# Expert outputs of a mixture layer: two accumulators by column halves in place of two by block parity

## The reference

```python
def expert_block(args):
    tok, e = args
    xb = x2d[tok]
    hb = jax.nn.silu(xb @ exp_w1[e]) * (xb @ exp_w3[e])
    return hb @ exp_w2[e]

yb = lax.map(expert_block, (slot_tok.reshape(NB, MOE_BLOCK), block_expert))
routed = jax.ops.segment_sum(yb.reshape(P, D) * slot_w[:, None].astype(x2d.dtype), slot_tok, num_segments=N)
shared = (jax.nn.silu(x2d @ shared_w1) * (x2d @ shared_w3)) @ shared_w2
return routed + shared
```

## Time and profile before

| | us |
|---|---|
| median of 3 runs | 2030.21 |
| lowest and highest | 2025.59, 2031.33 |
| the profiled execution | 2026.94 |
| its span, first to last instruction | 2025.1 |

### The profile page before, as it was taken

How to read it: one execution, slowest core, us unless ns; L and a number is a source line. 1 busy time by engine, 2 the same in 40 slices (tenths; PEclk the granted TensorE clock), 3 DMA queues, 4 the chain that set the end, 5 groups by cost and what they waited for, 6 DMA issues and landing times.

```text
span 2025.1 us, 34620 instructions
## 1 busy us (share of the span) xinstructions
PE 1843.0 (91%) x9251; PEld 1421.6 (70%) x9251; DVE 1491.4 (74%) x2060; ACT 1262.7 (62%) x1746; POOL 734.3 (36%) x754
## 2 busy tenths in 40 slices
PE   5787998999999899599999999999999999999950
PEld 2343444799888555387888888888888888888840
DVE  3367555532668668854999999999999999999946
ACT  3353545443224333334888888888888888888842
POOL 3211000000003114533455555555555555555532
PEclk8898999999999999799999999999999999999985
DMA  7733210234302322526886998976777878997977
GB/s 240 262 128 114 78 36 21 83 117 140 88 1 84 130 92 97 219 95 228 289 299 163 320 347 264 334 248 152 220 268 236 275 273 303 324 326 279 312 220 186
DMA packets 121260, 399.55 MB, mean 197 GB/s; under 512 B 28397, under 2 KB 52973, under 8 KB 96237
## 3 DMA queue, kind: packets, MB, share of 16 engines
q1 hardware_dynamic: 75644, 281.66, 37.6%
q0 software_dynamic: 45264, 117.06, 22.1%
q10 hardware_dynamic: 290, 0.02, 0.0%
HBM read 355.47 MB, written 84.60 MB: 217 GB/s over the span
## 4 chain that ended last, share of the span: by engine, by line
PE 49%; DMA 3%; DVE 2%; issue 1%; ACT 1%; POOL 1%; ACTq 1%; DVEq 0%; SPq 0%; POOLq 0%
PE bank L1989 28%; PE bank L2009 14%; PE bank L1976 5%; DMA y<-yacc_scratch 1%; PE bank L1996 1%; DMA big<-in_exp_w 1%; ACT wuph L2086 1%; DVE big L2296 1%; ACTq L1744 0%; POOL slot_table L1918 0%; DVE big L2288 0%; DVE wupl L2181 0%; DVE y L2287 0%; DMA yacc_scratch<-y,idx_s 0%; DMA xg<-hn_scratch 0%
## 5 line engine op out<-in xcount | busy, mean ns | idle before, releaser
L2181 DVE TENSOR_TENSOR wupl<-big,wuph 128x2048 fp32r<-128x2048 f32 x214 | 489.9, 2290 | 74.9 <-ACT wuph L2086 71.3
L2086 ACT ACTIVATE wuph<-big 128x2048 fp32r (+1 forms) x214 | 408.7, 1911 | 11.8 <-SPq L1807 7.1
L1989 PE MATMUL bank<-wuph,xTh 128*128 128x512 f32 x912 | 366.0, 401 | 7.2 <-DVE xTl L2203 6.8
L1989 PE MATMUL bank<-wuph,xTl 128*128 128x512 f32 x912 | 358.3, 393 | 0.0
L1989 PE MATMUL bank<-wupl,xTh 128*128 128x512 f32 x912 | 356.8, 391 | 0.0
L1910 POOL DMA_INDIRECT yacc_scratch<-y,idx_s x105 | 227.4, 2166 | 301.8 <-ACT y L2077 285.2
L1900 POOL DMA_INDIRECT xg<-hn_scratch,idx_g x108 | 237.0, 2194 | 117.5 <-issue 109.4
L2189 DVE TENSOR_TENSOR w2l<-w,w2h 128x1024 fp32r<-128x1024 f32 x212 | 249.7, 1219 | 8.8 <-ACT w2h L2095 8.4
L2095 ACT ACTIVATE w2h<-w 128x1024 fp32r (+1 forms) x212 | 213.1, 1053 | 69.0 <-issue 59.0
L1989 PEld LDWEIGHTS bank<-wuph,xTh 128*128 128x128 f32 x912 | 172.2, 189 | 44.2 <-issue 6.4
L1989 PEld LDWEIGHTS bank<-wuph,xTl 128*128 128x128 f32 x912 | 171.6, 188 | 37.1
(11 more groups left out here) (360 smaller groups left out, 3153.4 us busy)
## 6 DMA issues: line engine op xcount, KB each, us to landing
big<-in_exp_w SPq DMA_DIRECT2D x128, 1024.0 KB, 9.8
w<-in_exp_w SPq DMA_DIRECT2D x64, 1024.0 KB, 11.7
wada<-in_w_ada POOLq DMA_DIRECT2D x16, 1024.0 KB, 6.3
wg<-in_w_in SPq DMA_DIRECT2D x14, 1024.0 KB, 5.3
wada<-in_w_ada SPq DMA_DIRECT2D x4, 2048.0 KB, 14.6
big<-in_w_in SPq DMA_DIRECT2D x8, 1024.0 KB, 5.4
yacc_scratch<-in_consts SPq DMA_DIRECT2D x9, 512.0 KB, 9.7
x<-x_scratch SPq DMA_DIRECT2D x9, 512.0 KB, 4.1
```

What stands on the lines that cost most here:

```text
L1989: mm = pe.matmul(b_up[j][:, :], x[:, k, :], w[:, :, k, :], start=(k == 0 and i == 0), stop=(k == KT - 1 and i == 2))
L2086: act.activation(part13(wup[j][0], half), raw13(e % WSLOT, half), ACT.Copy).then_inc(w_high, 1)
L2181: dve.tensor_tensor(part13(wup[j][1], half), raw13(e % WSLOT, half), part13(wup[j][0], half).bitcast(F32), ALU.subtract).then_inc(w_low, 1)
```

## The change

The two accumulators become 1152 x 512: the first holds columns 0 to 511 of every token, the second columns 512 to 1023. Each block is scattered by two indirect DMAs, one per half. All blocks now add into both tensors, so each of these DMAs waits until the same half of the block before has landed. The shared expert's outputs are stored in halves too, and nothing is filled with zeros. At the end SP loads each tile in two halves, and there is no adding load. ACT waits for both halves before it writes `y[j]` again, and in its last block down_high goes ahead of ht.

```diff
-            for t in range(NT):
-                sp.dma_start(m.yacc[1][t * P:(t + 1) * P, :], a["consts"][:, C_ZERO:C_END]).then_inc(m.s_zero, 16)
...
+        COLS = [slice(h * 512, (h + 1) * 512) for h in range(2)]
...
-            sp.wait_ge(y_out[0], n * 16 + 16 * ((NSH + 1) // 2))
+            for h in range(2):
+                sp.wait_ge(y_out[h], n * 32 + 16 * (NSH + 1))
             for t in range(NT):
-                sp.dma_start(y6[t][:, :], m.yacc[0][t * P:(t + 1) * P, :]).then_inc(s_y[min(batch_of(t), 1)], 16)
+                for h in range(2):
+                    sp.dma_start(y6[t][:, COLS[h]], m.yacc[h][t * P:(t + 1) * P, :]).then_inc(s_y[batch_of(t)], 16)
...
             def store(b):
 
                 hold(y_act, b + 2)
-                pool.dma_start(m.yacc[0][b * P:(b + 1) * P, :], y[b % 2][:, :]).then_inc(y_out[b % 2], 16)
+                for h in range(2):
+                    if b >= 1:
+                        hold(y_out[h], 16 * b)
+                    pool.dma_start(m.yacc[h][b * P:(b + 1) * P, :], y[b % 2][:, COLS[h]]).then_inc(y_out[h], 16)
 
             def scatter(q, j):
                 hold(y_act, q + (NSH + 2))
-                pool.indirect_dma_start(m.yacc[j], bass.IndirectOffsetOnAxis(ap=idx_s[j][:, :], axis=0), y[j][:, :], None,
-                                        compute_op=ALU.add, bounds_check=N - 1, oob_is_err=False).then_inc(y_out[j], 16)
+                for h in range(2):
+                    hold(y_out[h], q * 16 + 16 * NSH)
+                    pool.indirect_dma_start(m.yacc[h], bass.IndirectOffsetOnAxis(ap=idx_s[j][:, :], axis=0), y[j][:, COLS[h]], None,
+                                            compute_op=ALU.add, bounds_check=N - 1, oob_is_err=False).then_inc(y_out[h], 16)
...
-            pool.wait_ge(m.s_zero, 16 * NT)
...
-                    hold(y_out[j], r * 16 + 16 * ((NSH + u) // 2))
+                    hold(y_out[1], (r * 2 + u) * 16 + 16 * (NSH - 1))
...
-            hold(y_out[1], n * 16 + 16 * ((NSH + 1) // 2))
-            for j, (t0, t1) in enumerate(YPARTS):
-                if j < 2:
-                    pool.wait_ge(s_y[j], 16 if j == 0 else 16 * (NT - 1))
-                for t in range(t0, t1):
-                    pool.dma_start(y6[t][:, :], m.yacc[1][t * P:(t + 1) * P, :], accum_op=ALU.add).then_inc(s_sum[j], 16)
...
-            def y_half(b, j, sent):
+            def y_half(b, j):
                 act.wait_ge(down_done, 2 * b + 2)
                 if not (isinstance(b, int) and b < 2):
-                    act.wait_ge(y_out[j], sent * 16)
+                    for h in range(2):
+                        act.wait_ge(y_out[h], b * 16 - 16)
...
+            down_high(n * 2 + NSH, n * 2)
             ht(n * 2 + NSH)
-            down_high(n * 2 + NSH, n * 2)
...
-                dve.wait_ge(s_sum[batch_of(t)], 16 * (t1 - t0))
+                dve.wait_ge(s_y[batch_of(t)], 32 * (t1 - t0))
...
-        m.yacc = [dram(f"yacc_scratch{j}", (N, D)) for j in range(2)]
+        m.yacc = [dram(f"yacc_scratch{h}", (N, D // 2)) for h in range(2)]
```

More of the change, by code:

```diff
@@ L57 @@
 C_TAB = C_COL + NE
-C_ZERO = C_TAB + 2 * NCOL
-C_END = C_ZERO + D
+C_END = C_TAB + 2 * NCOL
 def shape_constants():
@@ L85, in shape_constants @@
     col = np.concatenate([np.sin(ca), np.cos(ca)], -1).astype(np.float32)
-    slots = c[:, C_TAB:C_ZERO].view(np.int32).reshape(P, NCOL, 2)
+    slots = c[:, C_TAB:C_END].view(np.int32).reshape(P, NCOL, 2)
     slots[:, :, 0] = N + np.arange(P, dtype=np.int32)[:, None]
-    c[:, C_TAB:C_ZERO] = slots.reshape(P, 2 * NCOL).view(np.float32)
+    c[:, C_TAB:C_END] = slots.reshape(P, 2 * NCOL).view(np.float32)
     return c, row, col
@@ L530, in _ @@
         def _(sp):
-            sp.dma_start(m.table, a["consts"][:, C_TAB:C_ZERO].bitcast(I32).rearrange("p (c w) -> p c w", w=2)).then_inc(m.s_table, 16)
+            sp.dma_start(m.table, a["consts"][:, C_TAB:C_END].bitcast(I32).rearrange("p (c w) -> p c w", w=2)).then_inc(m.s_table, 16)
             for g in range(2, 6):
@@ L1712, in stage_experts @@
             "h_turned", "hT_ready", "down_done", "y_copied", "pool_step"))
-        y_out = [sem(f"y_sent{j}") for j in range(2)]
+        y_out = [sem(f"y_sent{h}") for h in range(2)]
+        COLS = [slice(h * 512, (h + 1) * 512) for h in range(2)]
         gathered = m.gathered
-        s_y, s_out = [sem(f"ld_y6_{j}") for j in range(2)], sem("st_y")
-        s_sum = [sem(f"sum_y6_{j}") for j in range(4)]
+        s_out, s_y = sem("st_y"), [sem(f"ld_y6_{j}") for j in range(4)]
         x_new, x_sq, y_new, rooted = (sem(n) for n in ("x3_new", "x3_sq", "y_new", "rooted"))
@@ L1950, in _ @@
                     scatter(r * 2 + u, j)
-            hold(y_out[NSH % 2], n * 16 + 16 * (NSH // 2))
+            hold(y_out[1], n * 32 + 16 * (NSH - 1))
             tokens(n * 2, idx_s[NSH % 2])
@@ L2127, in _ @@
                 if b >= 1:
-                    y_half(b - 1, (b - 1) % 2, (b - 1) // 2)
+                    y_half(b - 1, (b - 1) % 2)
                 silu(b + 1, (b + 1) % 2)
@@ L2142, in _ @@
                     high(r * 2 + (u + NSH + 2), j, r * 2 + (u + 2), HALVES[1:2])
-                    y_half(r * 2 + (u + NSH - 1), 1 - j, r + (u + NSH - 1) // 2)
+                    y_half(r * 2 + (u + NSH - 1), 1 - j)
                     silu(r * 2 + (u + NSH + 1), 1 - j)
                     xt(r * 2 + (u + NSH + 2), j)
+            down_high(n * 2 + NSH, n * 2)
             ht(n * 2 + NSH)
-            down_high(n * 2 + NSH, n * 2)
-            y_half(n * 2 + (NSH - 1), 1 - NSH % 2, n + (NSH - 1) // 2)
-            y_half(n * 2 + NSH, NSH % 2, n + NSH // 2)
+            y_half(n * 2 + (NSH - 1), 1 - NSH % 2)
+            y_half(n * 2 + NSH, NSH % 2)
             for i, (t0, t1) in enumerate(ROOTS):
@@ L2352, in program @@
         m.gathered = [sem(f"gathered{j}") for j in range(2)]
-        m.s_zero = sem("st_zero")
         m.at_xg = (nc.sbuf_usable_end - 8 * D) // 32 * 32
```

## The result

The changed kernel takes 2122.65 us (median of 4 runs, 2117.43 to 2130.98), the kernel before beside it 2027.9: a ratio of 1.0472 (95% interval 1.0441 to 1.0503). The forecast was 2055 with a range of 2003 to 2122. So the sign was right and the size was not: 95 us lost where the forecast, 2055 against a median of 2030, had 25. The profiled execution has a span of 2121.9 us.

The account below looks back on a forecast made before the run. It took PE to bound the expert stage, at 9.40 us a block. From 2026.94 us, +51 for the loop and -15 for the tail gave 2063, lowered to 2055 for fewer blocks in the stream; range 2003 to 2122.

Parts of the forecast that it names:

- The wait decides: Main loop: each half waits for the previous block's same half to land, setting the block at 10.67 us; chance 0.45.
- The loop's +51: Main loop: 74 us gross in the stream, less 3 of gather slack and 20 won back, net 51 us slower.
- The second DMA on POOL, 2.4 us, at no cost: Each block on POOL: the second scatter takes 2.4 us and fits in 2.83 us of idle time.
- the gather's 3 us of slack: Main loop: gathered rows land 3 us before the transposes need them, which takes up 3 us of loss, once.
- Landing of a half, 9.8 us: Scatter beside the weight stream: half a scatter lands in 9.8 us, between 8.8 and 11.4.
- 0.87 us of release: Main loop: 0.87 us from the release to the next scatter's issue, added to a half's landing.
- 58 blocks in the stream, less some 6 to 8: Main loop: 58 of 105 blocks run beside streaming weights, some 6 fewer (8 us) as the stage grows longer.
- 20 us won back in quiet blocks: Main loop: in 47 blocks without the weight stream POOL wins back 0.43 us each, 20 us.
- The tail's -15: After the last scatter: plain loads replace accumulating ones and the copies start sooner, 15 us saved, ends 10 and 18.
- POOL as pacemaker: Rival, main loop: a second scatter of 3.2 us makes POOL set 9.8 us a block throughout; 2105 us, chance 0.16.
- Hidden waits at 2012: Rival, main loop: halves land within 8.5 us even in the stream, only the tail counts; 2012 us, chance 0.27.
- The clock: Expert stage: the forecast fails if PE's waits lower its granted clock, 1.00 before; no size given.

Follow-up runs that it names:

- e2_whole: The changed kernel with one accumulator of whole rows, one scatter a block, each waiting for the block before to land; 2077.97 us, ratio 1.0253.
- e1_four: The changed kernel with four accumulators, by half and block parity: two scatters a block, no wait for the block before; odd routed blocks left out; 2062.74 us, ratio 1.0171.
- e3_half: The changed kernel with only the first half stored and scattered, columns 512 to 1023 left out; 2030.54 us, ratio 1.0022.
- e14_more_2k: e9_more_rows with the weight loads in four pieces of 2 KB; 2040.64 us, ratio 1.0071.
- e6_swap: The kernel before with ACT's last down_high ahead of ht in the last block, nothing else; 2027.67 us, ratio 1.0006.
- e4_after_few: The changed kernel with expert weight loads cut to an eighth of their bytes from the third expert on; 2006.89 us, ratio 0.9894.
- e9_more_rows: The kernel before with a second indirect DMA of 16 columns behind each scatter, into scratch, waiting only two blocks back; 2090.92 us, ratio 1.0307.
- e12_before_4k: The kernel before with the routed blocks' weight loads cut into two pieces of 4 KB; 2033.88 us, ratio 1.0039.
- e11_after_2k: The changed kernel with the routed blocks' weight loads cut into four pieces of 2 KB; 2027.25 us, ratio 1.0009.
- e5_before_few: The kernel before with expert weight loads cut to an eighth of their bytes from the third expert on; 2046.54 us, ratio 1.010.

## Why the prediction was right and wrong

**The wait decides: right in part.** POOL's idle time is ended by the landing of the scatter before, blocks start 11.3 us apart beside the weights, and PE waits for xg, as the prediction's last part said. But by e2_whole (whole rows) the wait is 64 of the 112 us; the other 48 are the second DMA's.

**The loop's +51 is the step that failed**; it was +112 against the measured 9.48. By its own terms (a block is in the stream here if SP's queue moved 200 GB/s or more from its scatter's start to the next):

- *The second DMA on POOL, 2.4 us, at no cost.* This is the term that was missing. It was set against POOL's idle time alone, 2.83 us a block (2.66 of it wait for y). The prediction says that the next gather moves later by the same 2.4 us, and yet counts the gather's 3 us of slack as still there, against the wait. Measured, the gather starts 3.7 us later with two DMAs (e1_four), of the slack 0.4 us is left, and the loop loses 48 us without any wait for the block before.
- *Landing of a half, 9.8 us.* In the stream the first half landed after 10.4 on average. In e3_half, without the other half, it is 9.7: the forecast fits a half that is alone. The reason given for the low end, that the gather's median holds its place behind a whole scatter, left out that the half has company too.
- *0.87 us of release.* In the rows above the next scatter starts 0.83 after the landing at best; in the stream it is 0.94 on average. So these blocks take 11.34 us, 1.94 over 9.40, where 1.27 was forecast.
- *58 blocks in the stream, less some 6 to 8.* There are 61.
- *20 us won back in quiet blocks.* Nothing was won back: the 43 other blocks take 9.44 on average. With one DMA a block there is something to win: in e3_half 61 blocks in the stream take 10.58, close to the forecast's 10.67, the 43 others 8.41, and the loop loses 21 us in all. With two DMAs the gather's slack is used up, so a late scatter makes PE idle, and time that PE has stood idle comes back only if PE has slack; it is full in the quiet stretch, 35.64 of 36.

So 61 x 1.94 + 43 x 0.04 = 120 over a loop of 9.40, and 112 over the measured 9.48.

**Why the landings are long.** The prediction named a rule for this, in the wait's term alone: by the Trainium skill ("DMA: Bandwidth & Descriptors", section "SWDGE vs HWDGE vs iDMA") an engine goes from queue to queue between packets. The runs with smaller pieces of weights agree with it in direction: beside weights in pieces of 8 KB the gather lands after 10.5 us (before), in pieces of 2 KB after 7.6 (e14_more_2k). A long landing is what makes POOL's delay and the wait cost time at all.

**The tail's -15.** From the last scatter to DVE's end it was 59.8 us before; the forecast has 46.7, and the changed kernel 2114.45 - 2069.59 = 44.9. The stores behind DVE take 1.6 of it back, so that 13.4 are left at the end of the span. The first tile's product comes 8.2 us sooner after the last scatter, where some 8 were forecast. Right. The 2.4 us by which the last scatter was to come sooner don't show: after the change it waited for a landing (2.06 us, in the rows of the tail), and alone, in e6_swap, the swap moves nothing.

**The rivals.** POOL as pacemaker came closest by its time, 2105, and is wrong by its mechanism: no even cadence (9.44 in quiet, 11.34 in the stream), and e4_after_few has all of POOL's work at 9.45. It was right that POOL's time counts, but it does so as a delay of the gather. Hidden waits at 2012 is what the kernel is without its weights (2006.89), or nearly with small pieces (2017.0); its condition, a half within 8.5 us in the stream, is not met by any of the seven halves above.

**The clock.** The prediction asked whether PE's waits lower it. The clock is a little lower: 0.98 over the stage, 1.00 before. PE's lines of the changed kernel, 1000 to 2020 us:

```profile
L2006 PE MATMUL bank<-w2h,hT5h 128*128 128x512 f32 x385 | 164.5, 427 | 0.0
...
L1973 PE MATMUL bank<-cst,xg 128*128 128x128 f32 x776 | 113.5, 292 | 85.2 <-DMA xg<-hn_scratch,idx_g 85.1
```

The same lines took 412 and 275 ns before. Whether PE's idle time is the reason is open: e9_more_rows, with PE busy for 885.51 of 940 us, has 1.00. The 21 us of added busy time bound the effect; PE is on 6% of the chain.

## What to carry to other kernels

Price an indirect DMA three times: by the time that it takes on its engine ahead of other DMAs (here the gathers), by the wait that hangs on its landing, and by what its rows do to the landings beside it. Fitting into an engine's idle time is not enough: the 2.5 us that a gather had left were gone after one more DMA ahead of it. Beside a stream of large pieces landings are long, so cutting a scatter in two can cost more than the halves save; cutting the stream's pieces instead gave most of it back. Spare time on a helper engine wins nothing back for a bound engine that is already full. And read a control in its trace: ten memsets were to stand for a second scatter and moved the next gather by 0.5 us, where the scatter moves it by 3.7.

## What the runs showed of the hardware

- 128 added rows of 64 bytes a block moved the landing of the scatter ahead of them from 11.4 to 14.3 us beside weights in pieces of 8 KB (1165 to 1235 us). The added DMA cost 64 us over 104 blocks there, and 12 together with pieces of 2 KB.
- A gather of 128 rows of 4 KB landed, beside weights in pieces of 8, 4 and 2 KB, after 10.5, 9.1 and 7.6 us (before, e12_before_4k, e14_more_2k). What the smaller pieces change inside the DMA engines is not shown. That the queues take turns piece by piece doesn't fit the counts: in microseconds with both queues at work (8 rows or more and over 200 KB of weights) some 36 pieces of 8 KB started beside 26 rows after the change, and 135 pieces of 2 KB beside 25 rows in e11_after_2k.
- The index copies on POOL took 1623 ns on average for idx_g after the change and 796 before, for the same copy; they stand ahead of the gather, so they have a share in its delay. And the kernel before became slower when seven eighths of its weight traffic were taken away (e5_before_few); the row that grew is known, its cause is not.
